# Experts of 129 to 140 slots: the down product with its weights standing, and the result transposed back

## The reference

```
gate = jax.nn.softmax(top_logit, axis=-1)            # top 4 of 32 per token
...
def expert_block(args):
    xb, e = args
    g = xb @ w_gate[e] + b_gate[e]
    u = xb @ w_up[e] + b_up[e]
    return clamped_swiglu(g, u) @ w_down[e] + b_down[e]

ys = lax.map(expert_block, (xs, block_e)).reshape(P, D)
ys = (ys.astype(jnp.float32) * slot_gate[:, None]).astype(h.dtype)
return jnp.zeros_like(h).at[slot_tok].add(ys)
```

## Time and profile before

| | us |
|---|---|
| median of three timed runs | 2295.27 |
| lowest and highest of them | 2294.91, 2297.12 |
| the profiled execution | 2290.64 |
| its span in the profile | 2288.9 |

### The profile page before, as it was taken

One profiled execution on the slowest core, in us unless ns is written; L12 is line 12 of the kernel. 1 busy time (PEld: TensorE's weight loads), 2 busy tenths in 40 slices (PEclk: granted clock), 3 DMA queues, 4 the chain that ended last, 5 costly groups with the idle time before them and its releaser, 6 DMA issues.

```text
span 2288.9 us, 36925 instructions
## 1 busy us (share of the span) xinstructions
PE 2222.8 (97%) x15112; PEld 1669.8 (73%) x15112; DVE 807.6 (35%) x2456; ACT 462.3 (20%) x1163; POOL 222.3 (10%) x262
## 2 busy tenths in 40 slices
PE   8998999999997799999999999999999999999997
PEld 4554666666664677888778887778878878878876
DVE  4555655555554222222222222222222222322222
ACT  3333544454443000000010000010000000000000
POOL 1000000000001111111112111110000000000000
PEclk9999999999999799999999999999999999999999
DMA  4000500000004887888878898879998998998971
GB/s 162 28 1 16 153 10 29 29 29 29 29 29 167 241 283 249 276 283 277 304 269 282 308 312 313 303 268 340 336 345 303 336 344 303 334 346 300 335 284 20
DMA packets 212027, 492.46 MB, mean 215 GB/s; under 512 B 23733, under 2 KB 27509, under 8 KB 211680
## 3 DMA queue, kind: packets, MB, share of 16 engines
q1 hardware_dynamic: 193552, 449.89, 54.4%
q0 software_dynamic: 16688, 40.02, 7.4%
q10 hardware_dynamic: 1616, 0.14, 0.1%
HBM read 464.68 MB, written 29.82 MB: 216 GB/s over the span
## 4 chain that ended last, share of the span: by engine, by line
PE 66%; DMA 0%; DVE 0%; issue 0%; POOL 0%; ACT 0%; SPq 0%; ACTq 0%; POOLq 0%
PE gu_bank L2019 42%; PE ya_bank L2033 19%; PE yb_bank L2046 3%; PE xa_bank L1989 1%; DMA biasT<-in_b_up 0%; PE xb_bank L1997 0%; POOL out_y L1762 0%; DVE xT L1906 0%; ACT y_rows L1832 0%; DVE y_rows L1895 0%; SPq L1685 0%; PE yb_bank L2060 0%; ACTq L1849 0%; PE yb_bank L2057 0%; DVE biasT L1947 0%
## 5 line engine op out<-in xcount | busy, mean ns | idle before, releaser
L2019 PE MATMUL gu_bank<-xT,ring_head 128*128 128x128 f32 (+10 forms) x4160 | 508.3, 282 | 2.6 <-DVE xT L1906 2.6
L2019 PEld LDWEIGHTS gu_bank<-xT,ring_head 128*128 128x128 f32 x4160 | 499.1, 192 | 11.6 <-issue 11.6
L2019 PE MATMUL gu_bank<-xT,ring 128*128 128x128 f32 (+8 forms) x4032 | 484.6, 280 | 0.0
L2019 PEld LDWEIGHTS gu_bank<-xT,ring 128*128 128x128 f32 x4032 | 476.8, 191 | 4.9 <-issue 4.8
L1872 DVE TENSOR_SCALAR g_in<-gu_bank,bias_cur 128x128 f32<-128x128 f32 (+10 forms) x256 | 91.9, 359 | 686.2 <-PE gu_bank L2019 686.2
L2033 PE MATMUL ya_bank<-ring,hidden 128*128 128x512 f32 x672 | 292.8, 594 | 0.0
L1826 ACT ACTIVATE sig<-g_in 128x128 f32<-128x128 f32 (+10 forms) x256 | 81.1, 317 | 870.7 <-DVE g_in L1872 870.7
L2033 PEld LDWEIGHTS ya_bank<-ring,hidden 128*128 128x128 f32 x672 | 126.0, 190 | 150.9 <-issue 147.8
L1895 DVE TENSOR_TENSOR y_rows<-ya_bank,b_row 128x512 f32<-128x512 f32 x64 | 41.2, 686 | 380.2 <-PE ya_bank L2033 380.2
L2033 PE MATMUL ya_bank<-ring_head,hidden 128*128 128x512 f32 x352 | 153.4, 594 | 0.0
L1762 POOL DMA_INDIRECT out_y<-y_rows,tab x31 | 49.9, 1609 | 905.1 <-ACT y_rows L1832 905.1
(11 more groups left out here) (331 smaller groups left out, 2032.2 us busy)
## 6 DMA issues: line engine op xcount, KB each, us to landing
ring<-in_w_down SPq DMA_DIRECT2D x42, 2048.0 KB, 12.5
ring_head<-in_w_up SPq DMA_DIRECT2D x33, 2048.0 KB, 10.3
ring_head<-in_w_gate SPq DMA_DIRECT2D x32, 2048.0 KB, 13.1
ring<-in_w_gate SPq DMA_DIRECT2D x32, 2048.0 KB, 13.1
ring<-in_w_up SPq DMA_DIRECT2D x31, 2048.0 KB, 11.3
ring_head<-in_w_down SPq DMA_DIRECT2D x22, 2048.0 KB, 12.9
b_row<-in_b_down SPq DMA_DIRECT2D x32, 512.0 KB, 10.0
xt<-in_x SPq DMA_DIRECT2D x8, 512.0 KB, 3.8
```

Of the source, the lines that this page charges most:

```text
L2019: last = nc.tensor.matmul(gu_bank[:, f % 2, i * 256:i * 256 + width], w[:, k, c * P:(c + 1) * P], xT[:, k, 0:width], start=(k == 0), stop= ...
```

## The change

In turns of 129 to 140 slots (`tall`: nine turns, the 7th to the 15th) the down product is turned round (`down_turned`). For each of 8 chunks c of 128 output features, 8 products accumulate in one of two halves of `ya_bank`: a 128 x 128 piece of the down weights stands, and all 130 to 140 slots of `hidden` move. The result has output features in its partitions. ScalarE copies it to `yT` (`results`). While the next chunk is multiplied, TensorE transposes the copy back (`turn_back`): the first 128 slots into `xa_bank`, the bank that the gathered tokens' transposes also use, and the slots above 128 into `yb_bank`. The pair of the last chunk stands in the next turn's gate and up, behind its first piece f = 0. VectorE adds the bias in two halves (`bias_turned`): the first after chunk 3's transposes, the second after chunk 7's; the narrow part of a half first, since `yb_bank` holds one half at a time.

The part above 128 slots now has its slots in partitions over all 1024 features (`y_turned`), so the adds need no worked out table (`to_row_b`), the bias no separate `b_more` (four small loads less per turn), and `tab_b` one load in place of four. `transpose_x` gets a wait for the bias sums that read `xa_bank`. A down chunk of the weights is free when the last of the eight products' groups is done. Eight semaphores of the first stage are replaced by those of the ring, and the counts of the ring's waits moved up for them.

```diff
@@ -1517,6 +1518,16 @@
     return sum(wide(a) for a in range(at))
 
 
+def tall(at):
+
+    return P < WIDTHS[at] <= TALL if at < TURNS else False
+
+
+def talls(at):
+
+    return sum(tall(a) for a in range(at))
+
+
 def parts(width):
 
     return 4 if width <= P + 32 else 2
...
@@ -1659,6 +1676,8 @@
                 def wait_free(at, c):
                     if c < 4:
                         sp.wait_ge(gu_done, at * FC + 4 * (c // 2 + 1))
+                    elif tall(at):
+                        sp.wait_ge(yt_done, (talls(at) + 1) * DC)
                     elif wide(at):
                         sp.wait_ge(yb_done, wides(at) + 1)
                     elif c == 4:
...
@@ -1673,7 +1692,7 @@
                             sp.wait_ge(biased_b, wides(at - 1))
                     sp.dma_start(b_row[:, at % 2, :], io["b_down"][bass.ds(e, 1), :].rearrange("one d -> (one d)")
                                  .partition_broadcast(P)).then_inc(b_here[at % 2], 16)
-                    if wide(at):
+                    if wide(at) and not tall(at):
                         n = parts(WIDTHS[at])
                         q, c = P // n, D // n
                         for j in range(n):
...
@@ -1749,7 +1768,7 @@
                     slots(b % 2, rows_of(b), b)
                     pool.wait_ge(tab_in, 16 * b)
                     if wide(b):
-                        loads[0] += 16 * parts(WIDTHS[b])
+                        loads[0] += 16 * (1 if tall(b) else parts(WIDTHS[b]))
                         pool.wait_ge(tab_b_in, loads[0])
                     pool.wait_ge(x_done, 2 * b)
                     if wides(b):
...
@@ -1764,7 +1783,14 @@
                         out_offset=bass.IndirectOffsetOnAxis(ap=tab[:, i, 0:1] if b else keep["first_tab"][:, 0, 2:3], axis=0),
                         in_=y_rows[:], in_offset=None, bounds_check=row_last, oob_is_err=True,
                         compute_op=ALU.add).then_inc(added, 16)
-                    if wide(b):
+                    if tall(b):
+                        n = WIDTHS[b] - P
+                        pool.wait_ge(yb_out, wides(b) + 1)
+                        pool.indirect_dma_start(
+                            out=io["acc"], out_offset=bass.IndirectOffsetOnAxis(ap=tab_b[0:n, i, 0:1], axis=0),
+                            in_=y_turned[0:n, :], in_offset=None, bounds_check=row_last, oob_is_err=True,
+                            compute_op=ALU.add).then_inc(added_b, 16)
+                    elif wide(b):
                         n = parts(WIDTHS[b])
                         nc.gpsimd.tensor_scalar(to_row_b[:, i:i + 1], tab_b[:, i, 0:1] if b else keep["first_tab"][:, 1, 2:3], masks[:, 0, b:b + 1],
                                                 masks[:, 1, b:b + 1], ALU.mult, ALU.add).then_inc(masked, 1)
...
@@ -1827,11 +1853,20 @@
                             .then_inc(sig_ready, 1)
 
                 def results(b, at, i):
+                    if tall(at):
+                        for c in range(DC):
+                            act.wait_ge(yt_done, talls(at) * DC + c + 1)
+                            nc.scalar.copy(yT[:, c, 0:WIDTHS[at]], ya_bank[:, c % 2, 0:WIDTHS[at]]).then_inc(yt_out, 1)
                     for h in range(2):
                         act.wait_ge(biased, b * 2 + (h + 1))
                         nc.scalar.activation(y_rows[:, h * 512:(h + 1) * 512], y_rows[:, h * 512:(h + 1) * 512], ACT.Copy,
                                              scale=gate_of(i, at)).then_inc(y_out, 1)
-                    if wide(at):
+                    if tall(at):
+                        n = WIDTHS[at] - P
+                        act.wait_ge(biased_b, wides(at) + 1)
+                        nc.scalar.activation(y_turned[0:n, :], y_turned[0:n, :], ACT.Copy,
+                                             scale=tab_b[0:n, i, 1:2].bitcast(F32)).then_inc(yb_out, 1)
+                    elif wide(at):
                         n = D // parts(WIDTHS[at])
                         act.wait_ge(biased_b, wides(at) + 1)
                         nc.scalar.activation(y_more[:, 0:n], y_more[:, 0:n], ACT.Copy,
...
@@ -1883,6 +1918,22 @@
                             dve.wait_ge(g_sig_ready, b * FC + f)
                             v.scalar_tensor_tensor(hidden[:, s, 0:width], u_in[:, s % 2, 0:width], 1.0 - LIMIT,
                                                    g_sig[:, s % 2, 0:width], ALU.max, ALU.mult).then_inc(hidden_ready, 1)
+
+                def bias_turned(at, loads):
+
+                    n, i = WIDTHS[at] - P, at % 2
+                    dve.wait_ge(b_here[i], 16 * loads)
+                    dve.wait_ge(added, at * 16)
+                    dve.wait_ge(added_b, 16 * wides(at))
+                    for h in range(2):
+                        c = slice(h * 512, (h + 1) * 512)
+                        if h:
+                            dve.wait_ge(ya_done, at + 1)
+                        else:
+                            dve.wait_ge(yr_half, talls(at) + 1)
+                        v.tensor_tensor(y_turned[0:n, c], yb_bank[0:n, :], b_row[0:n, i, c], ALU.add)\
+                            .then_inc(biased_b if h else yb_half, 1)
+                        v.tensor_tensor(y_rows[:, c], xa_bank[:, h, :], b_row[:, i, c], ALU.add).then_inc(biased, 1)
 
                 def bias_rows(b, at, loads, more):
                     dve.wait_ge(ya_done, b + 1)
...
@@ -1983,6 +2037,8 @@
                     pe.wait_ge(x_in, b * 16 + 16)
                     if at:
                         pe.wait_ge(x_out, b * 2)
+                    if 2 <= at < TURNS + 2 and tall(at - 2):
+                        pe.wait_ge(biased, 2 * (at - 1))
                     for h in range(2):
                         for k in range(4):
                             c = (4 * h + k) * P
...
@@ -2020,6 +2076,41 @@
                                                         w[:, k, c * P:(c + 1) * P], xT[:, k, 0:width],
                                                         start=(k == 0), stop=(k == DC - 1))
                         last.then_inc(gu_done, 1)
+                        if f == 0 and 1 <= at < TURNS and tall(at - 1):
+                            turn_back(at - 1, DC - 1)
+
+                def turn_back(at, c):
+
+                    n, h = WIDTHS[at] - P, c // 4
+                    cols = slice(c % 4 * P, (c % 4 + 1) * P)
+                    pe.wait_ge(yt_out, talls(at) * DC + c + 1)
+                    if c == 0:
+                        pe.wait_ge(x_out, 2 * (at + 2))
+                        pe.wait_ge(biased_b, wides(at))
+                    if c == 4:
+                        pe.wait_ge(yb_half, talls(at) + 1)
+                    nc.tensor.transpose(xa_bank[:, h, cols], yT[:, c, 0:P], ident[:])
+                    last = nc.tensor.transpose(yb_bank[0:n, cols], yT[:, c, P:P + n], ident[:])
+                    if c % 4 == 3:
+                        last.then_inc(ya_done if h else yr_half, 1)
+
+                def down_turned(at):
+
+                    pe.wait_ge(biased, at * 2)
+                    wait_weights(at, 4, 0)
+                    wait_weights(at, 5, 0)
+                    for c in range(DC):
+                        if c >= 2:
+                            pe.wait_ge(yt_out, talls(at) * DC + c - 1)
+                        for k in range(FC):
+                            if c == 0:
+                                pe.wait_ge(hidden_ready, at * FC + (k + 1))
+                            last = nc.tensor.matmul(ya_bank[:, c % 2, 0:WIDTHS[at]],
+                                                    down_part(at, k // 4)[:, k % 4, c * P:(c + 1) * P],
+                                                    hidden[:, k, 0:WIDTHS[at]], start=(k == 0), stop=(k == FC - 1))
+                        last.then_inc(yt_done, 1)
+                        if c:
+                            turn_back(at, c - 1)
 
                 def down(b, at, more):
                     if at:
...
@@ -2063,7 +2154,10 @@
                     gate_up(at, at, WIDTHS[at], 0)
                     if at + 1 < TURNS:
                         transpose_x(at + 1, at + 1)
-                    down(at, at, 0)
+                    if tall(at):
+                        down_turned(at)
+                    else:
+                        down(at, at, 0)
                 pe.wait_ge(left_ready, 1)
                 left = pe.value_load(left_n[0:1, 0:1], min_val=0, max_val=LEFT)
                 with pe.If(0 < left):
```

More of the change, by code:

```diff
@@ L56 @@
 RING = 9
+TALL = 140
 HEAD = 4
@@ L165, in project @@
         w_hi_in = [m.sem(f"w_hi_in{k}") for k in range(DC)]
-        w_lo_in = [m.sem(f"w_lo_in{k}") for k in range(DC)]
+        w_here = keep["w_here"]
         gains_set = m.sem("gains_set")
@@ L263, in _ @@
                 for k in range(DC):
-                    sp.dma_start(w_in[:, k, 0:C_K], io["w_in"][0, k * P:(k + 1) * P, 0:C_K]).then_inc(w_lo_in[k], 16)
```

(22 more changed lines are left out.)

## The result

| | median us | lowest and highest |
|---|---|---|
| before, 4 runs | 2295.09 | 2294.07, 2297.12 |
| changed, 4 runs | 2320.39 | 2317.52, 2323.67 |

The ratio is 1.0112, 95% interval 1.0098 to 1.0125: the change makes the kernel 1.1% slower, 25.3 us by the medians. The profiled execution took 2323.67 us, its span 2321.7.

A forecast was written before the change was run, and what follows sets the result against it. TensorE, busy 97% of the span, was taken to bound the kernel. New gather waits of 17.5 us less 9.1 saved gave +8.4: 2299.0 us profiled, 2304 as median; the 8-in-10 range was 2287 to 2320.

The forecast's parts named there:

- What TensorE saves, 9.1 us: Nine turns of 130 to 140 slots: turned products plus transposes back replace 17.52 us of down product each, saving 9.1 us.
- transposes that don't overlap: Rival: each transpose back shows its whole 0.273 us, +23.6 on TensorE, +14.5 after the saving, 2310 us; chance 0.05.
- When the gather lands, S + 31.7: S starts gate and up behind a down product; add at 6.3, then 10.6 to table read, 6.5 to gather, 8.3 landing.
- The forecast's upper bound for this, 12.2: On GpSimd, the longest time assumed from first add to table read: 12.2 us, a second add under load.
- Waits of 17.5 us: TensorE waiting for late gathers after gate and up: 1.0, 3.7, 10.8 and 2.0 us, together 17.5.
- the 4.0 that one row had shown: On GpSimd, table read to gather in the two turns that fetch a narrow turn, without tab_b: 4.0 us.
- Forecast: 17.5 - 9.1 = +8.4 us: Whole kernel: TensorE's new gather waits less its saved work, giving 2304 us as the median.
- Gathers in time: Rival: gathers land at 29.0 us after gate and up starts, no wait left, -9.1, 2286 us; chance 0.21.
- Long waits: Rival: add, table read and gather all at their long ends, 43.4 us of waits, +34, 2330 us; chance 0.08.
- a lateness of 7.5: Add of a turned down product's result, issued 6.3 us after gate and up starts instead of 1.2 before: 7.5 us later.

The follow-up runs named there:

- early fetch: Changed kernel, but GpSimd reads the slot table and gathers turn b + 2's tokens ahead of turn b's adds, with a third table buffer: 2286.39 us, ratio 0.9957.
- the run that fills the waits: Changed kernel with 12 useless products before the gathered tokens' transposes that follow a turn of 129 to 140 slots: 2309.5 us, ratio 1.0074.

## Why the prediction was wrong

The sign was right, and so were the waits for the gathers and their place. The size was a third: +8.4 us forecast, +25.3 measured, and the range ended at 2320, 0.4 us under the median. A second cost behind each wait, the clock, was left out of the sum.

- **What TensorE saves, 9.1 us.** Right. The chain has 1.80 us for a group of 16 instructions at 132 columns (1.81 taken) and 0.22 for a pair of transposes back, twice the assumed 0.109. The early fetch shows the sum: 9.8 us in the ten turns, 9.9 by the ratio (6.7 to 13.1 by its interval). The upper bound, transposes that don't overlap, was not approached. Each transpose lasts 0.273 us here too but the next one starts earlier, and ScalarE's copy of 0.27 us is hidden behind a group, as argued (columns: times, busy us, mean ns, idle before):

```profile
L2092 PE MATMUL xa_bank<-ident_sb,yT 128*128 128x128 f32 x72 | 19.6, 273 | 0.0
...
L2093 PE MATMUL yb_bank<-ident_sb,yT 128*4 128x128 f32 x32 | 8.7, 273 | 0.0
...
L1859 ACT COPY yT<-ya_bank 128x132 f32<-128x132 f32 x32 | 8.6, 268 | 77.9 <-PE ya_bank L2108 77.9
```

- **When the gather lands, S + 31.7.** Right by its parts in the turn shown above: first add S + 6.2 (6.3 forecast), from there to the table read, issued at 1333.07, 10.8 us (10.6), to the gather 7.0 (6.5), landing 7.4 (8.3), together S + 31.4. In all nine turns the table read came 10.6 to 12.0 us behind the first add. The forecast's upper bound for this, 12.2, was counted from the second add of its row; from the first, at 1537.98, that turn had 15.3. For all nine the landing was:

```profile
DMA to landing us min/median/max: 6.6/7.7/8.2
```

  The gathers of the same turns in the kernel before had a median of 8.7, so these landed somewhat sooner, while the table reads took longer, a median of 5.7 us against 5.0. The Trainium skill's fit for one DMA (DMA: Bandwidth & Descriptors, Anatomy of one DMA) gives an estimate of 3.2 us for this gather; the shortest of these nine took 6.6.
- **Waits of 17.5 us.** 20.7 to 22.5 measured. The four waits behind gate and up at 132 columns sum to 9.9 us (10.8 forecast). The two behind 136 columns were 2.9 and 2.3 us, where 1.85 was put. The two turns that fetch a narrow turn waited 1.5 and 3.1 us, where 1.0 was put: in the second of them (S = 1568.49) the table read came 12.0 us behind the first add and the gather 5.5 behind the read, not the 4.0 that one row had shown.
- **The step that failed** is the sum itself, "Forecast: 17.5 - 9.1 = +8.4 us". It prices a wait of TensorE at its length and puts the clock behind it at nothing, without a reason. The runs showed 14 to 15 us there, nearly as much as the waits: 14.7 in the five stretches at half clock, and 13 to 14 by the run that fills the waits. That term alone would have made the forecast some +23. No wait of 1 to 3 us stood in these turns before, so no row there priced it. One row ahead of the first turn shows the size of such a loss, but not that a short wait brings it: the eight transposes of the first turn took 1.97 us, not the 1.04 that this view (timeline of the kernel before) has for them elsewhere. There the granted clock had been 0.50 since 743.6, long before TensorE stood for the gather.

```profile
763.54 1.97 PE L1989 MATMUL xa_bank<-ident_sb,x_rows 128*128 128x128 f32 x8 [7.52 <-DMA x_rows<-ffn_rows,first_tab]
```

  The Trainium skill (TensorE: Matmul & The Clock Gate, Why this matters for your kernels) lists idle gaps between bursts as what brings the clock to its lower level. The trace agrees in five of nine waits, and with the waits filled the clock stays at 1.00. Why four waits kept the full clock, one of them 3.1 us long, no run here shows.
- **The rivals.** Gathers in time: out in the changed kernel, and its number, 2286, is the value of the change with the early fetch. Transposes that don't overlap: out, by 0.22 us a pair. Long waits: its time of 2330 was nearer than the forecast, but by luck, since the waits came to 21 us and not to 43.

## What to carry to other kernels

A change that saves work on the critical engine can lose more on the path of the results that it now hands on later. Trace each result of the changed piece forward to what the critical engine takes next, and write down the slack of that transfer, which no list of waits shows (here 1.65 us against a lateness of 7.5). Where a buffer or a table can be doubled so that a fetch doesn't queue behind a store, do that first. And price a new wait of TensorE at its length plus what the clock may take behind it, here two thirds more.

## What the runs showed of the hardware

- Waits of TensorE of 1.7, 2.3, 2.6, 2.9 and 3.2 us each went with a stretch of 3.4 to 6.8 us at half clock, 1.7 to 3.4 us lost each time; waits of 1.0, 1.5, 2.4 and 3.1 us in the other four turns kept the full clock. With useless products in the same place the stretch of all nine turns reads 1.00.
- An indirect add of 2 to 12 rows of 4 KB, issued 1.9 us behind one of 128 rows, took 7.3 to 8.8 us to land (nine of them), in the changed kernel. In the kernel before, the one in its place, of 128 rows of 1 KB, took 7.2 to 9.2.
- A transpose back that keeps 2 to 12 columns and one that keeps 128 each take a step of 0.11 us in the chain; in both, 128 columns move.
